# The decode rows of a hybrid decoder layer: projected in column groups between the levels of the last prompt tile

## The reference, cut to what matters

```python
h = rmsnorm(x, norm1) * (1 + sc1) + sh1            # sc, sh, g: adaLN rows of the sequence
q, f_pre, i, g, v = split(h @ w_in)                # 1024 -> 5 * 512
f = lb + (1 - lb) * sigmoid(f_pre); k = 1 - f      # 4 heads of 128
S_t = diag(f_t) S_{t-1} + k_t outer i_t;  o_t = S_t^T silu(q_t)
o_a = rmsnorm_per_head(o) * silu(g)
o_b = pooled(v) @ w_pool * pool_scale              # trailing means over 2, 4, 8, 16 rows
x = x + g1 * (concat(o_a, o_b) @ w_out)
h2 = rmsnorm(x, norm2) * (1 + sc2) + sh2
x = x + g2 * moe(h2)                               # top 4 of 32 experts
```

## Time and profile before

| | |
|---|---|
| Median of 3 runs | 2424.58 us (2423.91 to 2425.52) |
| The profiled execution | 2420.09 us, its span 2418.5 us |
| PE busy in the span | 2199.9 us (91%) |
| DVE, ACT, POOL busy | 1603.8, 1261.3, 661.8 us |
| First level of the last prompt tile starts | 602.48 us |
| x1 of the last prompt tile is complete | 677.72 us |
| The table of work items is complete | about 781.3 us |

### The profile page before, as it was taken

The page is one execution under the profiler, slowest core; times in us unless marked ns, Lnnn a source line. Parts: engine busy times, 40 slices in busy tenths (PEclk is TensorE's granted clock), DMA queues, the critical chain, the costliest instruction groups (busy, mean ns, idle before and its releaser), DMA issues. The chain is left out here.

```text
span 2418.5 us, 38959 instructions
## 1 busy us (share of the span) xinstructions
PE 2199.9 (91%) x12114; PEld 1595.9 (66%) x12115; DVE 1603.8 (66%) x2240; ACT 1261.3 (52%) x1662; POOL 661.8 (27%) x936
## 2 busy tenths in 40 slices
PE   6999999999975589999999999999999999999945
PEld 5767777766942467667676667777676676776631
DVE  2345445444225678778787669988797697997647
ACT  1233333333220457657665658767676666785532
POOL 2222342332131313222322223232232232333200
PEclk8999999999586799999999999999999999999975
DMA  9760000000021888779787769998898798997616
GB/s 373 283 229 36 9 26 35 35 33 31 5 69 41 339 307 288 275 272 348 262 312 285 270 239 322 383 328 328 295 371 312 255 353 312 342 372 290 234 31 236
DMA packets 143746, 554.10 MB, mean 229 GB/s; under 512 B 20832, under 2 KB 35437, under 8 KB 109317
## 3 DMA queue, kind: packets, MB, share of 16 engines
q1 hardware_dynamic: 118175, 496.69, 53.7%
q0 software_dynamic: 23680, 51.82, 9.2%
q10 hardware_dynamic: 1838, 4.93, 0.6%
HBM read 512.31 MB, written 41.25 MB: 229 GB/s over the span
## 5 line engine op out<-in xcount | busy, mean ns | idle before, releaser
L1765 DVE TENSOR_TENSOR lo<-raw,hi 128x1024 fp32r<-128x1024 f32 x800 | 930.7, 1219 | 173.7 <-ACT hi L1693 171.9
L1693 ACT ACTIVATE hi<-raw 128x1024 fp32r<-128x1024 f32 x800 | 791.5, 1049 | 98.1 <-PE pg L1608 92.1
L1605 PE MATMUL pg<-hi,xs 128*128 128x512 f32 x1056 | 424.8, 402 | 0.8 <-DVE lo L1765 0.8
L1606 PE MATMUL pg<-lo,xs 128*128 128x512 f32 x1056 | 416.1, 394 | 0.0
L1608 PE MATMUL pg<-hi,xs 128*128 128x512 f32 x1056 | 332.3, 396 | 0.0
L1605 PEld LDWEIGHTS pg<-hi,xs 128*128 128x128 f32 x1056 | 198.9, 188 | 75.5 <-issue 16.6
L1540 PE MATMUL py<-hi,aT 128*128 128x512 f32 x528 | 221.6, 420 | 11.8 <-ACT aT L1705 4.9
L1608 PEld LDWEIGHTS pg<-hi,xs 128*128 128x128 f32 x1056 | 198.7, 188 | 48.1
L1606 PEld LDWEIGHTS pg<-lo,xs 128*128 128x128 f32 x1056 | 199.0, 188 | 43.9
L345 PE MATMUL X<-hT,w_in 128*128 128x128 f32 (+1 forms) x1728 | 226.0, 291 | 0.8 <-issue 0.8
L345 PEld LDWEIGHTS X<-hT,w_in 128*128 128x128 f32 x1728 | 221.5, 210 | 1.2 <-issue 1.2
(11 more groups left out here) (320 smaller groups left out, 2794.3 us busy)
## 6 DMA issues: line engine op xcount, KB each, us to landing
raw<-in_w_gu SPq DMA_DIRECT2D x268, 1024.0 KB, 10.5
raw<-in_w_down SPq DMA_DIRECT2D x132, 1024.0 KB, 9.9
w_out<-in_w_ada SPq DMA_DIRECT2D x10, 2048.0 KB
w_in<-in_w_in SPq DMA_DIRECT2D x5, 2048.0 KB, 18.5
moe_rows<-small SPq DMA_DIRECT2D x9, 512.0 KB, 9.2
w_in<-in_w_ada SPq DMA_DIRECT2D x2, 2048.0 KB
xr<-in_x_prompt SPq DMA_DIRECT2D x8, 512.0 KB, 3.7
w_out<-in_w_out SPq DMA_DIRECT2D x1, 4096.0 KB, 13.8
```

The source lines that it names most:

```text
L1605: pe.matmul(pg[u][b][:, :], xs[:, kt, 0, :], wh[:, u, :], start=False, stop=False)
L1606: pe.matmul(pg[u][b][:, :], xs[:, kt, 0, :], wl[:, u, :], start=False, stop=False)
L1693: act.activation(hi[q % RING][:, :, :], grain(q % GRAINS), ACT.Copy).then_inc(s["hi"], 1)
L1765: dve.tensor_tensor(lo[q % RING][:, :, :], grain(q % GRAINS), hi[q % RING][:, :, :].bitcast(F32), ALU.subtract).then_inc(s["lo"], 1)
```

## The change

The sample gets buffers of its own, cut out of those parts of `w_in` whose projection is already done (`sample`, chosen by `of(T)`), its own banks for its levels (`lvl_ps_s`: X3 and T1), and loads of its states, residual rows and adaLN rows straight into further parts of `w_in`, issued by SP as soon as the second and the fourth of five projections are done (semaphore `sam_mm`). `tile(TILES - 1, NS)` is replaced on each engine by an order written out by hand, in which t is the last prompt tile and u the sample.

The sample is projected by `project_sample`: the 32 rows of h are the stationary operand, each of the four column groups of the array takes 128 of the 512 weight columns, and the results stand in the bank in four groups of 32 partitions. f, q and v are then turned by one transposition each (`turn`, after a copy by ACT into `row0` to `row2`). The output projection (`project_out_sample`) and the mixing with the states (`mix_sample`) use the four groups too.

```diff
+            def project_sample(bank, first):
+                for kt in range(KT):
+                    for g in range(H):
+                        last = pe.matmul(bank[g * NS:(g + 1) * NS, 0:P], hT[:, kt * NS:(kt + 1) * NS], w_in[:, kt, first + g * P:first + (g + 1) * P],
+                                         start=(kt == 0), stop=(kt == KT - 1))
+                last.then_inc(s["sam_mm"], 1)
+
+            def turn(j, bank, name):
+                pe.wait_ge(s["row_s"], j + 1)
+                pe.transpose(bank[:, 0:P], sample[f"row{j}"], ident[:, :]).then_inc(s[name], 1)
...
+            def project_out_sample(t):
+                pe.wait_ge(s["oT"], t + 1)
+                pe.wait_ge(s["pool_y"], t + 1)
+                pe.wait_ge(s["x1"], t)
+                W = D // H
+                for kt in range(KT):
+                    for g in range(H):
+                        last = pe.matmul(X0[g * NS:(g + 1) * NS, 0:W], sample["mixT"][:, kt * NS:(kt + 1) * NS], w_out[:, kt, g * W:(g + 1) * W],
+                                         start=(kt == 0), stop=(kt == KT - 1))
+                last.then_inc(s["out_mm"], 2)
...
-            tile(TILES - 1, NS)
...
+            level(t, P, 2)
+            pe.wait_ge(s["v"], t + 1)
+            project_sample(X2, 4 * HW)
+            level(t, P, 3)
+            turn(0, X0, "f_mm")
+            pe.wait_ge(s["gs"], t + 1)
+            project_sample(X3, 2 * HW)
...
+            level(t, P, 7)
+            transpose_k(t, P, T0)
+            mix(t, P, LV)
+            pe.wait_ge(s["vtc"], 1)
+            pooling(t, P)
+            pe.wait_ge(s["sgf"], u + 1)
+            pe.wait_ge(s["vx"], u + 1)
+            level(u, NS, 0)
+            transpose_o(t, P)
+            pe.wait_ge(s["q"], u + 1)
+            project_out(t, P)
...
+            pe.wait_ge(s["lg"], u)
+            pe.wait_ge(s["rank_used"], u)
+            route(u, NS)
+            rank(u, NS)
...
+            weigh(t, P)
+            states(0, NB // 2)
+            norm_out_sample()
+            place(t, P)
+            states(NB // 2, NB // 2)
+            h2_high(u, T)
+            logits(u, T)
...
+            h2_low(u, T)
+            act.wait_ge(s["vrow"], 2)
             act.dma_start(out["H_p"][0, 0], x[P - HIST:P, HW:D]).then_inc(s["vrow_out"], 16)
...
             for j in range(NB):
                 act.dma_start(out["H_s"][0, j, HIST - TS:HIST, :], x[j * TS:(j + 1) * TS, 0:HW]).then_inc(s["vrow_out"], 16)
-            norm_out(t, T)
-            h2_low(t, T)
-            soften(t, T)
+            soften(u, T)
```

More of the change, by code:

```diff
@@ L428, in mix_sample @@
                     for m in range(H):
-                        last = pe.matmul(bank[:, m * P:(m + 1) * P], kT[0:T, m * P:(m + 1) * P], Vz[:, j, m * P:(m + 1) * P], start=True, stop=True)
+                        last = pe.matmul(bank[:, m * P:(m + 1) * P], sample["kT"][0:NS, m * P:(m + 1) * P], Vz[:, j, m * P:(m + 1) * P], start=True, stop=True)
                     last.then_inc(s["S_s_mm"], 1)
@@ new lines, in _ @@
+            level(t, P, 3)
+            turn(0, X0, "f_mm")
+            pe.wait_ge(s["gs"], t + 1)
+            project_sample(X3, 2 * HW)
+            level(t, P, 4)
+            turn(1, X1, "q_mm")
+            project_sample(T1, 3 * HW)
+            level(t, P, 5)
+            turn(2, X2, "v_mm")
+            level(t, P, 6)
+            pe.wait_ge(s["hist_in"], 16)
+            pe.wait_ge(s["v"], u + 1)
+            for m in range(H):
+                last = pe.transpose(X3[:, m * NB * HIST:(m + 1) * NB * HIST], hist[:, m * P:(m + 1) * P], ident[0:NB * HIST, 0:NB * HIST])
@@ new lines, in _ @@
+            last.then_inc(s["hist_ps"], 1)
+            level(t, P, 7)
+            transpose_k(t, P, T0)
+            mix(t, P, LV)
[7 more added lines that the diff above has]
+            project_out(t, P)
+            pe.wait_ge(s["gs"], u + 1)
+            level(u, NS, 1)
+            transpose_k(u, NS, T0)
@@ new lines, in _ @@
+            level(u, NS, 2)
+            pe.wait_ge(s["pool_y"], u)
+            pooling(u, NS)
+            pe.wait_ge(s["lvl"], u * LV + 2)
+            rank(t - 1, P)
+            mix_sample(u, len(BLOCKS_S) + 1)
+            pe.wait_ge(s["rank_used"], t)
+            pe.wait_ge(s["kT"], u + 1)
+            route(t, P)
+            transpose_o(u, NS)
+            project_out_sample(u)
+            rank(t, P)
+            states_sample(u)
+            for m in range(H):
+                last = pe.transpose(L0[:, m * P:(m + 1) * P], vx[:, m, HIST:HIST + P], ident[:, :])
@@ L568, in load_row, with norm @@
                 act.dma_start(dst[:, :], mod[0:1, m * D:(m + 1) * D].broadcast_to([P, D])).then_inc(s[name], 16)
-            def norm(src, T, col, done, tag):
-                act.activation(junk[0:T, :], src, ACT.Square,
+            def norm(src, T, col, done, tag, waste=None):
+                ss, rs = (prompt if waste is None else sample)["ss"], (prompt if waste is None else sample)["rs"]
+                act.activation(junk[0:T, :] if waste is None else waste, src, ACT.Square,
                                accum_out=ss[0:T, col:col + 1]).then_inc(s["ss" + tag], 1)
@@ L583, in h_low, with levels @@
                 act.activation(hT[:, 0:4 * T], T0[:, 0:4 * T], ACT.Copy).then_inc(s["hT_lo"], 1)
-            def levels(t, T, blocks):
+            def levels(t, T, blocks, between=()):
+                lv = of(T)["lev"]
                 for i in range(len(blocks)):
                     act.wait_ge(s["dlev"], t * (LV - 1) + i + 1)
-                    act.activation(lev[i % 2][:, 0:H * T], lev[i % 2][:, 0:H * T], ACT.Exp).then_inc(s["elev"], 1)
+                    act.activation(lv[i % 2][:, 0:H * T], lv[i % 2][:, 0:H * T], ACT.Exp).then_inc(s["elev"], 1)
+                    if i < len(between) and between[i]:
+                        between[i]()
                     if first_tile(t) and i and BEFORE + i <= len(PANELS):
@@ L657, in norm_out @@
                 act.wait_ge(s["x1"], t + 1)
-                norm(xr[0:T, :], T, 1, t + 1, "2")
+                if T == P:
+                    norm(xr[0:T, :], T, 1, t + 1, "2")
+                else:
+                    norm(xr_s, T, 1, t + 1, "2", junk_s)
             def h2_low(t, T):
@@ L673, in tile @@
                 o_cols(t, P)
[L674 to L677 removed]
+                keep_v(t + 1)
                 decays(t + 1, next_T)
@@ L773, in invert @@
             def invert(T, c, n, tag, done):
+                rs = (sample if T == NS and tag != "1" else prompt)["rs"]
                 dve.wait_ge(s["root" + tag], done)
```

414 lines of the change are left out of this document (242 added, 172 removed).

## The result

| | before | changed |
|---|---|---|
| median of 5 runs, us | 2423.91 (2418.2 to 2425.52) | 2435.39 (2429.08 to 2439.74) |
| ratio | | 1.0059, 95% interval 1.0044 to 1.0074 |
| span of the profiled execution | 2418.5 | 2438.1 |
| store of the item table (end of the mixing) | 781.34 | 713.43 |
| from there to the end of the span | 1637.2 | 1724.7 |

The account below looks back on a forecast made before the run. A serial tail from the last prompt tile's levels to the item table, with no engine full, was taken to bound it. Savings of 23.8 + 43.6 = 67.4 us, less 0.6 kept back, took 2424.58 to 2358 us; range 2345 to 2383.

Parts of the forecast that it names:

- groups that do not overlap: Rival: column groups run serially, each sample projection four times as long, 14.3 us at low clock; 2455 us, chance 0.03.
- Levels 22.2: Last prompt tile's eight levels with five sample projections between them: 22.2 us instead of 40.95.
- The clock rose where it was expected: PE's clock in the levels: up some 4 us into them and staying up; 0.78 for levels at full clock.
- To the output projection 11.6: From the end of the levels to the last prompt tile's output projection: 11.6 us instead of 16.95.
- the wait for DVE's pooling scale: Last prompt tile's output projection starts at about 636, behind DVE's pooling scale, delayed by 3.3 us of sample work.
- Output projection and residual 17.6: Last prompt tile's output projection and residual, starting at low clock: 17.6 us, against 17.34 before; x1 complete at 653.9.
- Behind x1 60.0: From the last prompt tile's x1 to the table of work items: 60.0 us instead of 103.62, 43.6 less.
- the sample's output projection: Behind x1, in column groups on PE: 3.8 us at full and 7.3 at half clock, taken as 5.4; 15.71 before.
- the issue on ACT: ACT's issue of the history rows, 3.18 us, now ahead of the sample's softmax: at most 0.3 us of cost.
- 2.9 us of projection and level: In the levels, PE's 2.9 us of work matches a level's 2.9 us over DVE, ACT and POOL; one 1.3 us wait.
- 0.95 for faster: Chance that the whole kernel gets faster by more than about 0.2% (5 us); within 0.02, slower 0.03.

Follow-up runs that it names:

- the loop moved on: Sixteen empty instructions on DVE ahead of its expert loop, in its wait for the table, against the changed kernel: 2355.32 us, ratio 0.9733 to the kernel before.
- The run in turn: Kernel with forty empty DVE instructions, both grouped projections reordered so each column group's eight products stand together: 2376.17 us, 28.3 us more than its base.
- places 0 and 128: Shift of DVE's expert loops against the changed kernel: 0 is that kernel (2435.39 us), 128 adds 128 empty DVE instructions (2436.79 us).
- places 0 and 8: Shift of DVE's expert loops against the changed kernel: 0 is that kernel (2435.39 us), 8 adds eight empty DVE instructions (2502.39 us).

## Why the prediction was wrong

**The step that failed** stands in its first paragraph: "Everything behind the table (experts, combination) is left as it is, so what this stretch loses the kernel loses, one for one." The source was left as it is; its place in DVE's instruction stream was not. Four instructions more, ahead of a nest of loops whose middle one stood on its last good place and whose innermost one three places from its border, cost 87.5 us in the profiled execution (1724.7 against 1637.2), more than the 67.9 us that the table came earlier; 87.5 - 67.9 is the 19.6 us by which the spans differ. With the loop moved on, the kernel takes 2355.32 us, and the forecast was 2358.

**No rival held it.** The one slower case, groups that do not overlap, was the wrong mechanism, and its price was too high: 28.3 us as measured, against 97 in the prediction (2455 - 2358), which counted four times the time at the low clock, and had the mixing with the states in turn as well; that was not tried. The run in turn had a factor of three, at full clock.

**The terms of the sum.** Levels 22.2, measured 21.79 by the cut of the earlier trace rows. The clock rose where it was expected: windows of 4 us, the granted clock in the column behind POOL's,

```profile
598.00:602.00 4.00, 3.57 (x21) 3.40 (x21) 1.59 (x6) 1.79 (x3) 2.73 (x3) 0.50 0.02 1
602.00:606.00 4.00, 4.00 (x73) 3.48 (x73) 1.10 (x3) 1.29 (x3) 3.27 (x4) 0.70 0.02 4
606.00:610.00 4.00, 4.00 (x95) 3.56 (x97) 1.73 (x4) 0.91 (x2) 1.41 (x2) 1.00 0.02 4
```

from 0.50 to 1.00 during the first projection, and it stayed there up to the last level (1.00 from 618 to 622). To the output projection 11.6, measured 12.67, with the wait for DVE's pooling scale as named (3.09 us). Output projection and residual 17.6, measured 16.94. Behind x1 60.0, measured 61.00; inside it two terms were 3.2 us too small and others, not taken apart here, too large: the sample's output projection 6.56 instead of 5.4, and the issue on ACT, which was to cost at most 0.3 and left a wait of 2.33 us. The issue took 4.17 us where the earlier trace rows has 3.18, and the table load behind it, 1.28 us, was named but not priced.

**Right for a partly wrong reason.** The prediction set 2.9 us of projection and level against 2.9 us of a level's way over the other engines, as if each projection filled a wait of its own. Taken out of the gaps they cost 4 us, not 9.5: one wait of 1.98 us and the low clock behind it. Most of the levels' way was hidden without them.

**Chances.** 0.95 for faster rested on rows of one phase only. The pages of the phase that was "left as it is" had the clue: a DVE loop of 269 instructions that made no fetch at all, with nothing known of how near it stood to the edge. The forecast of the mixing phase was sound in its mechanism, but that it came within 1 us is in part luck: its four stages were off by -0.4, +1.1, -0.7 and +1.0 us, and the last of these hides 3.2 that were missing.

## What to carry to other kernels

A change ahead of a long loop moves that loop in the engine's instruction stream, on every engine that it gives or takes an instruction. Where the loop's length is near what the engine holds, look at the page's line for the instruction queue and at "issue" idle at the loop's first operation before judging the change; a kernel with a handful of empty instructions ahead of the loop tells in one run whether a loss (or a gain) belongs to the change or to the place. The count matters: eight made this kernel 67 us worse, where sixteen mended it. Place the whole nest of loops, not the innermost one alone, and make that run a part of comparing any two versions.

## What the runs showed of the hardware that I had not expected

- DVE's stream is fetched in pieces of 8.2 KB, with a pattern that repeats every 128 instructions (places 0 and 128 behave alike). A loop over two borders made no fetch; over three, 4 to 5 transfers per item and stops of 5.06 us in the mean at the branch back, with the DMA engines busy for 0.76 to 0.92 of the stop, and 2.74 to 3.54 us where they were busy for 0.01 to 0.03.
- A border within the loop's head costs a further 2.94 us in the mean, 35 times. Of the 62 us between places 0 and 8, 51 lie in the items and 12 behind the last of them.
- Column groups of 32 give a factor of 3.05 (5.95 to 1.95 us) at full clock when neighbours in the queue belong to different groups, against each group's products in a row.
- Sixteen empty instructions on DVE take 0.17 us and 128 take 3.4; eight small DMA issues on ACT take 3.18 us before and 4.17 in the changed kernel.
